# Gated delta scan: products of a step in another order, fewer projection pieces inside it, first convolution taps on ScalarE, two-input SiLU products in other places

## What is computed

```python
qkv = silu(dwconv_centred(qkv, conv_a_w, conv_a_b))      # 4 taps, one weight per channel
def step(s, xs):                                         # per chunk, each direction
    v_new = u_c - w_c @ s
    o_c = qg_c @ s + qk_c @ v_new                        # both products go to one output
    s = s * dl_c + kd_c.T @ v_new
o = rmsnorm(o_f + flip(o_b)) * silu(z)
```

## Time and profile before

| | |
|---|---|
| time, median of 3 runs | 1761.44 us (1755.57 to 1765.13) |
| the profiled execution's own time | 1763.63 us |
| its span | 1761.8 us |
| mean granted clock of PE | 0.975 of full speed |
| busy in the span | PE 92%, DVE 59%, ACT 43%, POOL 18% |
| front stage, heads | from 131.27 us (DVE's first instruction of head 0) to about 988 us |

### The profile page before, as it was taken

How to read it: one execution, slowest core, us unless ns; L and a number is a source line. 1 busy time by engine, 2 the same in 40 slices (tenths; PEclk the granted TensorE clock), 3 DMA queues, 4 the chain that set the end, 5 groups by cost and what they waited for, 6 DMA issues and landing times. The chain is left out here.

```text
span 1761.8 us, 24738 instructions
## 1 busy us (share of the span) xinstructions
PE 1628.5 (92%) x9814; PEld 1508.3 (86%) x9814; DVE 1045.4 (59%) x1766; ACT 758.4 (43%) x1600; POOL 317.5 (18%) x240
## 2 busy tenths in 40 slices
PE   7789899898989989899898599999999999999997
PEld 2579799898978989889777499999999999999986
DVE  1668768597776967768683464346534661154434
ACT  4344464544545445563443356535663551121211
POOL 1131121121221112121010111112111112224110
PEclk9889999999999999999999799999999999999999
DMA  9020212011120211112031111212121253153223
GB/s 326 25 58 25 66 28 89 19 38 66 44 76 16 64 41 53 67 28 89 5 123 40 52 59 56 69 50 69 56 69 50 69 167 118 36 190 114 86 72 120
DMA packets 115853, 127.25 MB, mean 72 GB/s; under 512 B 6461, under 2 KB 97430, under 8 KB 115738
## 3 DMA queue, kind: packets, MB, share of 16 engines
q1 hardware_dynamic: 115594, 125.60, 22.2%
q10 hardware_dynamic: 144, 0.07, 0.0%
HBM read 105.56 MB, written 20.09 MB: 71 GB/s over the span
## 5 line engine op out<-in xcount | busy, mean ns | idle before, releaser
L106 PE MATMUL mb<-h_hi,s_w_hi 128*128 128x384 f32 x1104 | 373.6, 338 | 5.0 <-POOL s_w_lo L1590 3.4
L108 PE MATMUL mb<-h_hi,s_w_lo 128*128 128x384 f32 x1104 | 370.7, 336 | 0.0
L107 PE MATMUL mb<-h_lo,s_w_hi 128*128 128x384 f32 x1104 | 370.7, 336 | 0.0
L106 PE MATMUL db<-h_hi,d_w_hi 128*128 128x384 f32 x792 | 288.1, 364 | 6.4 <-ACT padded_rows L502 3.4
L107 PE MATMUL db<-h_lo,d_w_hi 128*128 128x384 f32 x792 | 270.5, 342 | 0.0
L108 PE MATMUL db<-h_hi,d_w_lo 128*128 128x384 f32 x792 | 270.2, 341 | 0.0
L1590 POOL TENSOR_TENSOR s_w_lo<-s_w,s_w_hi 128x1024 fp32r<-128x1024 f32 x48 | 129.0, 2690 | 498.7 <-ACT s_w_hi L1615 498.7
L106 PEld LDWEIGHTS mb<-h_hi,s_w_hi 128*128 128x128 f32 x1104 | 207.2, 188 | 7.6 <-POOL s_w_lo L1590 4.3
L107 PEld LDWEIGHTS mb<-h_lo,s_w_hi 128*128 128x128 f32 x1104 | 207.2, 188 | 1.1
L108 PEld LDWEIGHTS mb<-h_hi,s_w_lo 128*128 128x128 f32 x1104 | 207.2, 188 | 0.0
L106 PEld LDWEIGHTS db<-h_hi,d_w_hi 128*128 128x128 f32 x792 | 151.9, 192 | 7.3 <-ACT padded_rows L502 3.7
(11 more groups left out here) (289 smaller groups left out, 2848.5 us busy)
## 6 DMA issues: line engine op xcount, KB each, us to landing
d_w<-in_w_in SPq DMA_DIRECT2D x34, 512.0 KB, 4.4
d_dt<-decay_rows SPq DMA_DIRECT2D x16, 576.0 KB, 5.5
d_qg<-decay_rows SPq DMA_DIRECT2D x16, 512.0 KB, 7.6
s_w<-in_w_gate SPq DMA_DIRECT2D x16, 512.0 KB, 4.3
s_w<-in_w_in SPq DMA_DIRECT2D x14, 512.0 KB, 4.0
branch_a<-d_kq SPq DMA_DIRECT2D x8, 576.0 KB, 3.3
branch_b<-l_z SPq DMA_DIRECT2D x8, 576.0 KB, 2.8
merge_gates_b<-l_gates SPq DMA_DIRECT2D x8, 576.0 KB, 5.5
```

Of the source, the lines that this page charges most:

```text
L106: pe.matmul(out, hi, rhi, start=(k == 0), stop=False)
L107: pe.matmul(out, hi, rlo, start=False, stop=False)
L108: return pe.matmul(out, lo, rhi, start=False, stop=(last and stop))
```

## The change

1. **Order of a step.** Before: `p1`, `qg`, `outputs(s-1)`, slot, `p2`, slot, `p3`. After: `p1`, slot, `p2`, `qg`, `p3`, `outputs(s)`. Step 0: `p2`, slot, `p3`, `outputs(0)`.
2. **Pieces of z.** One slot a step (`slots = STEPS`, 9) with 12 pieces in place of 16: 1, 1, 2, 1, 1, 2, 1, 1, 2 of them in steps 0 to 8. Four pieces of group 0 now run ahead of `mt`, between the query projection and the wait for `w2` (in the last head they run inside `mt`, with two others). Group 0 is finished two portions earlier, and the two portions freed take the first four pieces of group 1.
3. **First taps on ACT.** `first_tap(h+1, s)` is an ACT activation (Identity with scale and bias per channel, 1155 columns), for k behind `next_key`, for v behind `next_value`, for q in step 0. DVE starts with tap 1 and waits for `tap0`.
4. **Places on DVE.** `silu(h+1, 0)` moves from ahead of step 0 to behind `vk` of step 0. The query taps 1, 2 and 3 are one in each of the steps 3, 4 and 5.

```diff
+            def first_tap(h, s):
+                dst, c, src = (k2[:, h % 2, :], v2[:, :], q2[:, :])[s], QKV[s], row_of(h - 1, s)
+                par = lambda a: R.par[:, PA_CONV + (a * 3 + c) * H + h:PA_CONV + (a * 3 + c) * H + h + 1]
+                act.wait_ge(S["proj_out"], (block_of(h - 1, s) + 1) * NG)
...
+                act.activation(dst, src[:, 0:CONV], ACT.Identity, scale=par(0), bias=par(4)).then_inc(S["tap0"], 1)
...
                 next_key(h, 2)
                 if not last:
+                    first_tap(h + 1, 0)
                     high(block_of(h, 2))
                 for g in range(NG):
                     next_value(h, g)
+                if not last:
+                    first_tap(h + 1, 1)
                 high(block_of(h, 3))
...
                         decays(h + 1, 2 * s + 1)
-                        if s == 1:
+                        if s == 0:
+                            first_tap(h + 1, 2)
+                        elif s == 1:
                             silu_tanh(h + 1, 1)
...
+                if not last:
+                    project(block_of(h, 3), 0, range(0, 4))
                 pe.wait_ge(S["uz"], (h + 1) * Q)
...
-                        project(block_of(h, 3), 0, range(0, 2))
+                        project(block_of(h, 3), 0, range(0 if last else 4, 6))
...
-                project(block_of(h, 3), 0, range(2, 4))
+                project(block_of(h, 3), 0, range(6, KT))
...
-                project(block_of(h, 3), 0, range(4, 6))
+                project(block_of(h, 3), 1, range(0, 2))
...
-                project(block_of(h, 3), 0, range(6, KT))
+                project(block_of(h, 3), 1, range(2, 4))
...
-                units = [(g, k) for g in range(1, NG) for k in range(KT)]
-                slots = 2 * STEPS
+                units = [(g, k) for g in range(1, NG) for k in range(KT)][4:]
+                slots = STEPS
...
-                        if s == 1:
-                            pe.wait_ge(S["qg"], (h + 1) * DIRS)
-                            pe.wait_ge(S["o0"], h + 1)
-                        for d in range(DIRS):
-                            t = step_tile(s, d)
-                            pe.matmul(bank[(t - 1) // 4][:, (t - 1) % 4 * P:((t - 1) % 4 + 1) * P], qg[:, d, t, :],
-                                      state[:, d, :], start=(s == 1), stop=False, skip_group_check=True)
-                        if s > 1:
-                            outputs(s - 1)
-                    fill(2 * s)
+                    if s:
+                        fill(s)
                     for d in range(DIRS):
...
-                    fill(2 * s + 1)
+                    if s == 0:
+                        fill(s)
+                    else:
+                        if s == 1:
+                            pe.wait_ge(S["qg"], (h + 1) * DIRS)
+                            pe.wait_ge(S["o0"], h + 1)
+                        for d in range(DIRS):
+                            t = step_tile(s, d)
+                            pe.matmul(bank[(t - 1) // 4][:, (t - 1) % 4 * P:((t - 1) % 4 + 1) * P], qg[:, d, t, :],
+                                      state[:, d, :], start=(s == 1), stop=False, skip_group_check=True)
                     if s < STEPS - 1:
                         for d in range(DIRS):
...
-                    if s == 0:
-                        outputs(0)
-                outputs(STEPS - 1)
+                    outputs(s)
...
                 if not last:
-                    conv(h + 1, 0, range(TAPS))
+                    conv(h + 1, 0, range(1, TAPS))
                 for d in range(DIRS):
                     scaled_queries(d)
                 if not last:
-                    conv(h + 1, 1, range(TAPS))
-                    silu(h + 1, 0)
+                    conv(h + 1, 1, range(1, TAPS))
...
                     if not last:
-                        if s == 2:
+                        if s == 0:
+                            silu(h + 1, 0)
+                        elif s == 2:
                             silu(h + 1, 1)
-                        elif s in (3, 4):
-                            conv(h + 1, 2, ((0, 1), (2, 3))[s - 3])
+                        elif s in (3, 4, 5):
+                            conv(h + 1, 2, (s - 2,))
```

More of the change, by code:

```diff
@@ L218, in front_stage @@
         S = {n: sem("d_" + n) for n in (
-            "w_in", "w_hi", "w_lo",  "proj_mm", "proj_out", "clear", "taps", "silu_t", "silu", "sq_q", "ssq_mm", "ssq",
+            "w_in", "w_hi", "w_lo",  "proj_mm", "proj_out", "clear", "taps", "tap0", "silu_t", "silu", "sq_q", "ssq_mm", "ssq",
             "kt", "ssk", "kn", "ssk4", "nc", "root", "kk", "u", "bf", "bb", "bin", "uz", "x_set", "sol", "t1", "t2",
@@ L539, in z_out @@
                 evac(block_of(h, 3), g, row_of(h, 3))
+            def first_tap(h, s):
+                dst, c, src = (k2[:, h % 2, :], v2[:, :], q2[:, :])[s], QKV[s], row_of(h - 1, s)
+                par = lambda a: R.par[:, PA_CONV + (a * 3 + c) * H + h:PA_CONV + (a * 3 + c) * H + h + 1]
+                act.wait_ge(S["proj_out"], (block_of(h - 1, s) + 1) * NG)
+                if s == 0 and h >= 2:
+                    act.wait_ge(S["ov"], (h - 1) * STEPS * DIRS)
+                elif s == 1:
+                    act.wait_ge(S["vt_mm"], h * NG)
+                elif s == 2:
+                    act.wait_ge(S["qg"], h * DIRS)
+                    act.wait_ge(S["kq_mm"], h * NG)
+                act.activation(dst, src[:, 0:CONV], ACT.Identity, scale=par(0), bias=par(4)).then_inc(S["tap0"], 1)
             def silu_tanh(h, s):
@@ L1063, in conv @@
                 for a in taps:
+                    if a == 1 and h:
+                        dve.wait_ge(S["tap0"], 3 * (h - 1) + s + 1)
                     if a == 0:
                         dve.wait_ge(S["proj_out"], (j + 1) * NG)
[L1066 to L1070, removed]
                         ins = dve.tensor_scalar(dst, src[:, 0:CONV], par(0), par(4), ALU.mult, ALU.add)
```

## The result

The changed kernel takes 1712.97 us (median of four runs, 1710.01 to 1715.09), the kernel before on the same chip 1762.2 (1755.57 to 1765.13): a ratio of 0.9725, 95% interval 0.9692 to 0.9757. The forecast was 1716 us. The profiled execution has a span of 1712.9 us against 1761.8 before, 48.9 less, where the sum had said 47 to 48.

What follows compares the result with a forecast made beforehand. PE's order bounds unfilled steps, DVE tap steps and the stretch ahead of step 0, a DVE-POOL collision three heads. Seven heads 29, three excesses 12, last head 6: 47 to 48 off 1763.6, 1716 us; own range 1710 to 1722, wider 1700 to 1738.

Steps and rivals of the forecast that it cites:

- Four pieces ahead of `mt`: `p2` 1.2 earlier: Ahead of `mt`: four pieces fill PE's 2.88 us idle gap, so `p2` of step 0 comes 1.2 us earlier.
- First taps: DVE saves 0.91 us each: k's worth nothing, v's and q's count; ACT takes 1.15, nothing on the path.
- The SiLU product behind `vk` loses by 0.15, and `vnu` follows at +19.97: Step 0: POOL's low part starts 0.15 us earlier, the product ends 1.2 behind it; 0.4 of 2.2 gained is kept.
- Rival (1): SiLU product beats POOL's low part in most heads: 1.7 us a head, 12 in all, 1704 us; chance 0.14.
- The order of a step: Gains 0.57 us from `vnu` of step 1, 2.7 over six steps (25.2 to 22.5), 0.4 in the last step.
- The last head: Without DVE work in its steps: six steps gain 3.9 us, step 1 0.3, the end 0.4, `mt` 1.6; together 6.2.
- The three excesses of 4.0: Collided heads 0, 3 and 6 become like the others, losing about 4 us excess each, 12 in all.
- Rival (2): `outputs` holds the next `p1`: 0.3 in each step costs 19 us, 1735; at its bound 1726; chance 0.20.
- The slack of 0.1: `outputs(s)`, waiting for its own step's `vn`, fits ahead of the next `p1` with 0.1 us to spare.
- Rival (3): Clock falls in the steps: decides from four slow steps a head on, with nine about 1840 us; chance 0.04.
- Rival (4): Little changes, as what PE and DVE save is waited off at step 0: 1750 us; chance 0.07.
- The argument on the clock: At `mt`: with the 2.88 us wait filled, the work behind runs at full clock, about 3.2 us instead of 4.57.

Runs made afterwards that it cites:

- run 4: Run 2 with z's pieces where they were before: none ahead of `mt`, 16 over the nine steps; 0.9752, 1717.07 us.
- run 2: Changed kernel with POOL's low part made to wait for the SiLU product of k; 0.9685, 1704.94 us.
- run 5: Changed kernel with z's pieces where they were before: none ahead of `mt`, 16 over the nine steps; 0.9745 of the kernel before.
- run 10: Changed kernel with k's first tap alone back on DVE; 0.9739 of the kernel before.
- run 9: Changed kernel with the three first taps back on DVE; 0.9805 of the kernel before.
- run 8: Changed kernel with k's SiLU product back ahead of step 0; 0.977 of the kernel before.
- run 3: Run 2 with z's pieces 1, 1, 0, 2, 2, 2, 2, 2, 0 over the steps of heads 0 to 6; 0.9629, 1695.71 us.
- run 6: Changed kernel with the old order within a step on PE, all else kept; 0.9895 of the kernel before.
- run 7: Kernel before with only the new order of a step on PE, 16 pieces of z in one slot a step; 0.9948.
- run 11: Run 3 with the value taps ahead of the scaled queries on DVE; 0.9606, 1689.55 us.
- run 1: The changed kernel again with no edit, on another chip; 0.9723 of the kernel before, 1711.91 us.

## Why the prediction was right

The time (1716 against 1712.97), its own range, the side and the leading mechanism were right. By the steps of the sum:

- *Four pieces ahead of `mt`: `p2` 1.2 earlier.* Right: +15.34 to +15.40 in six heads and in the last, against +16.56 to +16.99 wherever the clock had fallen. The exception is head 2 (+16.93), for which the forecast had no term. The overrun in head 0 was 0.1 and not 0.4. The step was priced on the kernel before, and its worth depends on the company: without the race (run 4 against run 2) the seven heads lose 7.7 us by the old placing, with it (run 5) 1.7, because there a late `p2` also wins the race. The last head adds 3.1 and 5.6.
- *First taps.* k nothing (run 10), v and q 0.91 each at their own places: measured 0.9 and 0.92 (run 9), though of v's only 0.5 reaches `vnu`. ACT's price was 1.34 for 1.15, and hidden.
- *The SiLU product behind `vk` loses by 0.15, and `vnu` follows at +19.97.* +19.96 to +20.01 in four heads. In heads 0 and 5 the decay rows came late, `vk` started only at +17.2 and +17.4, and `vnu` stood at +20.65 and +20.86. Rival (1) came true in one head, by 0.06. Run 2 shows that the collision is the cause, since both instructions take their own length as soon as one waits for the other's end; run 8 shows that the place behind `vk` is what removed the 4 us of a collided head. The Trainium skill, SBUF — State Buffer, section Who interferes with whom, says that whichever of two such instructions issues first has the shared ports for its whole length. The trace agrees, down to margins of 0.06 us, in every head of these runs.
- *The order of a step.* `vnu` of step 1 to `p1` of step 2: 2.36 measured (504.91 to 507.27), 2.23 said, 2.80 before. The six steps behind it: 3.40, 3.65, 3.84, 3.84, 3.72, 3.65, together 22.1 against 25.2; the sum had 22.5. Two steps with a tap came as said (3.84); the four others were said 0.10 to 0.12 too long. Where nothing runs on DVE, `p1` to `p2` is 1.01 in the step shown above, and the sum had 1.18. It had taken 0.58 for `p1` from the earlier trace rows, where `p1` follows a wait; straight behind another instruction its record is followed by the next after 0.40. The last step gave 0.37 of 0.4 (3.46 against 3.83).
- *The last head.* 2.87 and 3.39 where 2.98 and 3.51 were said; the chain of states gained 6.6 where 6.2 was said.
- *The three excesses of 4.0.* Right: on average the three gained 8.7 us, the four others 4.5, which leaves 4.2. The prediction expected no slow clock behind the shorter wait; one head, head 5, had it, as shown above.

Where it was off by a microsecond or two: the heads' ordinary gain was 4.5 and not 4.2, and 1.9 us were lost outside the heads, which the sum did not look at. Here luck helped: the heads together gained 3 us more than the sum said, and the loss outside hid most of that.

Rival (2), `outputs` holding `p1`, had the largest chance after the forecast and did not come: `p1` has no idle time in front in the steps of the last head. A record of PE is longer than its pitch, so this alone proves little, but the 0.93 from a state to the next `vnu`, unchanged from the kernel before, does. The slack of 0.1 held. (Such a step of the kernel before has one idle gap of 0.22 on PE and not two: the earlier trace rows shows it at both ends. The sum doesn't use it.) PE's pitches in such a step (0.40, 0.61, 0.44, 0.45, 0.52 and 0.45) make the 2.87, but PE alone does not set it: without the piece the chain of waits through DVE still takes 2.80 (run 3). Rival (3), a slow clock in four steps a head and more, did not come. The clock did fall at the turn from step 0 to step 1 in head 5, at next to no cost, and in the back substitution of head 2; in run 6 it fell inside steps too. Rival (4) did not come.

The argument on the clock was right for the place it spoke of, and incomplete. It took the wait of 2.88 ahead of `mt` as the cause. With that wait, the clock fell there in four to six of the seven heads of each of four kernels (the one before, runs 4, 5 and 7); without it, `mt` ran at full clock in every head of all the others. But the wait alone doesn't tell how long the slow stretch lasts (2.80 or 4.13 for the same 18 products), and it also fell in the back substitution, with no long wait ahead, in one or two heads each of the changed kernel's first profile and of runs 2, 10 and 11, for 1.57 us of `p2` each time. In head 5 of the changed kernel's first profile and of runs 2, 3 and 6 it fell in the scan behind a wait of 1.23 to 1.35 for `vk`; with waits of 1.24 and 1.28 there it did not fall in runs 1 and 10. What decides that stays open.

## What to carry to other kernels

When two engines race for a shared resource and the margin is a tenth of a microsecond, price both outcomes for each repetition, and ask what waits behind the loser: here the same collision cost 4 us a head ahead of `vk` and 1 to 1.7 in most heads behind it, and making one of the two wait for the other, or moving it a step on, cost nothing. Price the parts of a change together, because they are not a sum: an order of work worth 9 us alone was worth 30 inside the whole change. And once a chain is set by one engine's order in some steps and by another's in the rest, put the first engine's filler work into the steps that the other sets: moving pieces so gave 9 us (run 3).

## What the runs showed of the hardware

- Two DVE instructions of different kinds were held by POOL's subtraction: the SiLU product (up to 3.50 us for 1.35) and, in run 9, a convolution tap (6.30 for three, 4.33 alone). Both read two large tensors in SBUF. `vk` and `vnu`, which read one operand in PSUM and stand in the same stretch, kept their 0.60. The held SiLU product ended 1.21 to 1.23 us behind POOL's end in all thirteen cases of the two profiles of the changed kernel, so hardly any of its 1.35 us was done before.
- The granted clock fell to a mean of 0.70 over 5 us in which PE was busy throughout (5.00 of 5.00 us), with idle time of 1 us at most before it (head 2 of the changed kernel).
- A delay can shorten a head: with `p2` 1.6 us late, head 2 of the changed kernel won the race and had `vnu` 0.4 earlier than its neighbours.
- An Identity activation with a scale and a bias for each partition took 1.33 to 1.36 us for 1155 columns in the heads of the changed kernel, a tanh of the same size 1.15.
